# adaLN vectors computed piece by piece beside other work, norms and mixes taken block by block, in a two-layer SSD/attention trunk

## The chip, the core and the metric

The kernel runs on one core of a Trainium2 chip. The metric is the device time of one execution in microseconds (us), the median of several runs. Engines are named as in the profile: PE (matrix products), PEld (its weight loads), DVE, ACT and POOL (elementwise work), SP (issues the transfers); PEq, DVEq and so on are their instruction queues.

## The reference

A trunk of two layers over 512 tokens of width 1024, in float32. `c` is one conditioning vector.

```
c_act = silu(c)
for l in range(2):
    ada = c_act @ w_ada[l] + b_ada[l]                 # 1024 -> 6144
    sh1, sc1, g1, sh2, sc2, g2 = split(ada, 6)
    h = rms_norm(x, norm1_g[l]) * (1 + sc1) + sh1
    z, xbc, dt, q, k, v, gate_s, gate_a = split(h @ w_in[l])
    y_ssm = mamba2(z, conv(xbc), dt) @ w_ssm_out[l]
    y_att = diff_attention(q, k, v) @ w_attn_out[l]
    x = x + g1 * ((sigmoid(gate_s)*y_ssm + sigmoid(gate_a)*y_att) @ w_out[l])
    h = rms_norm(x, norm2_g[l]) * (1 + sc2) + sh2
    x = x + g2 * (relu(h @ w_ff1[l])**2 @ w_ff2[l])
return rms_norm(x, final_g)
```

## The kernel before

Everything is kept transposed: `x` is 8 blocks of 128 channels by 512 tokens. All large weights come as **units** of 1024x256 (1 MB each) in one stream, in the order of their use: bc (units 0 to 3), xs (4 to 11), gates, z and ssm-out, qkv, attention-out (AO, 4), out (WO, 4), feed-forward (FF, 4 rounds of 8: four units up, four down). 80 units a layer. SP loads a unit into `raw`, ACT rounds it into `w_hi` (`convert`), POOL computes the rest `w_lo` (`low`, four instructions), and PE does 48 matmuls of 512 columns: for each of 8 k blocks and each of 2 column blocks j, hi x hi, hi x lo and lo x hi (`unit_rows`). The raw, w_hi, w_lo and PSUM buffers have two slots, so `low` of unit n+2 follows its `convert`, which waits until PE has finished unit n. Every engine has its own program; what it does is in the written order, and semaphores join the programs. The outer loop over the layers is a loop in the program.

- **Prologue of each layer** (`start`): params and dt weights are loaded after the layer before has ended. ACT squares the 8 blocks of x, DVE adds them (`norm_sums`), PE sums over partitions (L424), POOL takes the power (L1478), PE spreads it (L430). Then the 24 adaLN pieces (1 MB each): DVE multiplies every other one by `c_act` and adds (L1130 and seven of L1134), and PE sums the columns of the result (L454); PE does the rest as row products out of `raw` (L448), whose rows ACT copies out (L772) and PE turns (L462). Then `norm` on DVE and ACT: `pre` (L1090), `h_hi` (L749), `h_lo` (L1095) for 8 blocks, with the dt product on PE (L471 to L473).
- **Conv** (bc and xs): for each unit ACT seeds (L791), DVE adds three taps for each of two blocks (L1187), ACT takes tanh (L797), DVE multiplies (`silu`, L1197). Before the first unit's taps DVE has the dt chain to do (L1147 to L1180: some 25 small instructions on 32 rows). In xs PE also turns the blocks (L416).
- **AO and WO**: DVE mixes the gated halves (L1430, L1433), and when all 8 blocks are mixed ACT and DVE split them into hi and lo; after WO all 8 blocks of x are summed, then squared, then added up, then normed.
- **FF**: ACT takes relu and its square, DVE squares again and forms `op_lo` (L1455, L1458) in the first half of a round; in the second half DVE adds to x (L1464).
- **End**: the last norm writes `y_out` (L1090), and one transfer of 2 MB takes it out.

## Time and profile before

| what | us |
|---|---|
| median of 3 runs | 2995.1 (2992.75 to 2997.93) |
| profiled execution: its own time | 3004.83 |
| profiled execution: span | 3003.0 |
| PE busy | 2574.0 |
| DVE busy | 1322.4 |
| POOL busy | 1086.1 |
| ACT busy | 960.4 |
| mean granted clock of PE | 0.914 |

Stages of layer 0 in the timeline of PE: prologue to 122; bc and xs to 278; SSD, z and ssm-out to about 730; attention to 1031; AO to 1077; WO to 1127; FF from 1147 to 1496. Layer 1 begins there, its first unit at 1610, and ends at 2978. The busy times are sums over the span; a busy engine is not always the one that is waited for.

### The profile page before, as it was taken

The page shows a single profiled execution, that of the slowest core. Times are in us where ns is not written, and L with a number is a line of the kernel's source. Part 1 is how long each engine was busy: PE and PEld are TensorE (multiplying, and loading weights), DVE is VectorE, ACT ScalarE, POOL GpSimd, SP SyncE. Part 2 cuts the span into 40 slices and gives each one's busy share as a digit, 9 for nine tenths or more (in the row PEclk, how much of TensorE's full clock was granted, in tenths as well). Part 3 has the DMA queues.
Part 4 walks back from the last instruction along what each step waited for, and adds up shares of the span by engine and source line. Part 5 has one row for each costly group of instructions (what it writes and reads, how often), then busy time and mean ns, then how long its engine had stood idle before and what let it go on. Part 6 is the DMA issues. An engine that isn't in the chain of part 4 may idle for free.

```text
span 3003.0 us, 36626 instructions
## 1 busy us (share of the span) xinstructions
PE 2574.0 (86%) x12200; PEld 2051.4 (68%) x12200; DVE 1322.4 (44%) x2019; ACT 960.4 (32%) x1532; POOL 1086.1 (36%) x825
## 2 busy tenths in 40 slices
PE   5798889788888697999977988988898877799997
PEld 2586667687666476888735866676776655688885
DVE  5654434332655326333366444433335552343333
ACT  1244332322544223222212443332334442232221
POOL 0244343334322144555402443433343222445552
PEclk9899989899989698999978999998999977899998
DMA  7421111122111121222273211011121111212221
GB/s 300 175 84 70 42 42 42 66 75 77 59 55 43 43 91 64 98 98 98 97 302 116 84 57 52 32 57 70 70 91 56 43 43 57 84 71 98 98 98 56
DMA packets 34516, 251.56 MB, mean 84 GB/s; under 512 B 3824, under 2 KB 4208, under 8 KB 4976
## 3 DMA queue, kind: packets, MB, share of 16 engines
q1 hardware_dynamic: 34416, 250.30, 22.8%
q8 instruction: 54, 0.88, 0.1%
q14 instruction: 46, 0.38, 0.0%
HBM read 244.00 MB, written 6.29 MB: 83 GB/s over the span
## 4 chain that ended last, share of the span: by engine, by line
issue 51%; POOL 23%; PE 11%; POOLq 9%; DVE 3%; DMA 2%; ACT 1%; DVEq 0%; PEld 0%; PEldq 0%; ACTq 0%; SPq 0%
POOL w_lo L1485 21%; POOLq L1487 7%; PE gemm L384 3%; PE gemm L385 2%; PE gemm L386 2%; PE aux L448 2%; DMA raw<-stream 2%; POOL y_tok L1526 1%; POOL smalls L1478 1%; DVE conv L1187 1%; POOL xdt L1517 1%; POOLq L1522 1%; PE aux L416 0%; POOLq L1518 0%; DVE pre L1090 0%
## 5 line engine op out<-in xcount | busy, mean ns | idle before, releaser
L1485 POOL TENSOR_TENSOR w_lo<-raw,w_hi 128x512 fp32r<-128x512 f32 x704 | 963.9, 1399 | 1590.0 <-ACT w_hi L732 1588.6
L384 PE MATMUL gemm<-h_hi,w_hi 128*128 128x512 f32 x1536 | 647.3, 421 | 37.9 <-POOLq L1487 10.1
L732 ACT ACTIVATE w_hi<-raw 128x2048 fp32r<-128x2048 f32 x176 | 336.6, 1914 | 939.9 <-PE gemm L386 849.3
L385 PE MATMUL gemm<-h_lo,w_hi 128*128 128x512 f32 x1536 | 614.1, 400 | 0.0
L386 PE MATMUL gemm<-h_hi,w_lo 128*128 128x512 f32 x1536 | 613.3, 399 | 0.0
L384 PEld LDWEIGHTS gemm<-h_hi,w_hi 128*128 128x128 f32 x1536 | 298.5, 194 | 135.5 <-issue 59.9
L384 PE MATMUL gemm<-op_hi,w_hi 128*128 128x512 f32 x896 | 362.4, 404 | 26.6 <-POOLq L1487 23.0
L385 PE MATMUL gemm<-op_lo,w_hi 128*128 128x512 f32 x896 | 359.5, 401 | 0.0
L386 PE MATMUL gemm<-op_hi,w_lo 128*128 128x512 f32 x896 | 358.3, 400 | 0.0
L385 PEld LDWEIGHTS gemm<-h_lo,w_hi 128*128 128x128 f32 x1536 | 298.8, 195 | 69.6 <-issue 12.0
L386 PEld LDWEIGHTS gemm<-h_hi,w_lo 128*128 128x128 f32 x1536 | 297.6, 194 | 65.4
L402 PE MATMUL gemm<-w_hi,h_hi 128*128 128x256 f32 x768 | 233.1, 304 | 1.6 <-issue 1.6
L403 PE MATMUL gemm<-w_hi,h_lo 128*128 128x256 f32 x768 | 227.6, 296 | 0.0
L404 PE MATMUL gemm<-w_lo,h_hi 128*128 128x256 f32 x768 | 227.1, 296 | 0.0
L384 PEld LDWEIGHTS gemm<-op_hi,w_hi 128*128 128x128 f32 x896 | 175.1, 195 | 67.5 <-issue 16.2
L386 PEld LDWEIGHTS gemm<-op_hi,w_lo 128*128 128x128 f32 x896 | 174.9, 195 | 37.9
L385 PEld LDWEIGHTS gemm<-op_lo,w_hi 128*128 128x128 f32 x896 | 175.2, 196 | 36.5
L1455 DVE TENSOR_TENSOR usq<-relu 128x512 f32<-128x512 f32 x64 | 93.0, 1453 | 196.7 <-ACTq L1026 191.4
L402 PEld LDWEIGHTS gemm<-w_hi,h_hi 128*128 128x128 f32 x768 | 158.9, 207 | 10.2 <-issue 9.8
L1187 DVE SCALAR_TENSOR_TENSOR conv<-gemm,cw,conv 128x511 f32<-128x511 f32 x144 | 107.8, 749 | 122.6 <-ACT conv L791 98.0
L403 PEld LDWEIGHTS gemm<-w_hi,h_lo 128*128 128x128 f32 x768 | 159.0, 207 | 0.4
L404 PEld LDWEIGHTS gemm<-w_lo,h_hi 128*128 128x128 f32 x768 | 157.9, 206 | 0.0
(171 smaller groups left out, 2861.3 us busy)
## 6 DMA issues: line engine op xcount, KB each, us to landing
raw<-stream SPq DMA_DIRECT2D x200, 1024.0 KB, 4.8
ada_raw<-stream SPq DMA_DIRECT2D x24, 1024.0 KB, 7.2
xsave<-x SPq DMA_DIRECT2D x2, 2048.0 KB, 12.6
x<-xsave SPq DMA_DIRECT2D x2, 2048.0 KB, 7.8
x<-xT SPq DMA_DIRECT2D x1, 2048.0 KB, 7.7
out<-y_out SPq DMA_DIRECT2D x1, 2048.0 KB, 6.3
dtw_raw<-dtw SPq DMA_DIRECT2D x2, 512.0 KB, 8.0
rope_cos<-ropes SPq DMA_DIRECT2D x2, 256.0 KB, 2.7
```

The lines of the kernel that those rows point to most:

```text
L384: mm(o, w_hi[:, slot, k, cols], hi[:, k, :], start=k == 0, stop=False)
L385: mm(o, w_hi[:, slot, k, cols], lo[:, k, :], start=False, stop=False)
L386: last = mm(o, w_lo[:, slot, k, cols], hi[:, k, :], start=False, stop=k == KB - 1)
L402: mm(o, h_hi[:, k, toks], w_hi[:, slot, k, :], start=k == 0, stop=False)
L403: mm(o, h_lo[:, k, toks], w_hi[:, slot, k, :], start=False, stop=False)
L404: last = mm(o, h_hi[:, k, toks], w_lo[:, slot, k, :], start=False, stop=k == KB - 1)
L448: last = mm(ab[2 + s][0:1, 0:UW], cact[:, k:k + 1], raw[:, s, k, :], start=k == 0, stop=k == KB - 1)
L732: A(w_hi[:, slot], raw[:, slot], ACT.Copy).then_inc(hi_ready, 1)
L1187: last = STT(conv[:, c, lag:S], gb[c][:, 0:S - lag], cw[:, bass.ds(block * CONV + (CONV - 1 - lag), 1)], conv[:, c, lag:S], ALU.mult, ALU.add)
L1455: TT(usq[:, j], relu[:, c], relu[:, c], ALU.mult)
L1485: gp.tensor_tensor(w_lo[:, slot, ks], raw[:, slot, ks], w_hi[:, slot, ks].bitcast(F32), ALU.subtract)
L1487: pool.drain().then_inc(lo_ready, 1)
```

## The change

The 48 adaLN pieces of the two layers leave the two prologues. Eight pieces of layer 0 (those of shift 1 and scale 1) stay in front: four are done by DVE (`ada_piece` of DVE), four by PE as products with the piece as the stationary operand (`ada_piece` of PE: 16 matmuls of one column). Ten pieces (`EARLY`) are done by DVE in the conv stage of layer 0, one after each of its first ten units; thirty (`LATE`: six of layer 0 and all 24 of layer 1) by DVE in AO and FF of layer 0, one after each unit. Each is loaded by SP in its turn among the units, after a wait for the DVE step that frees its buffer, and PE sums its columns (`ada_column`) in the middle of a later unit. A unit is now done column block by column block (`unit_column`) where its input is complete. Mixes, squares and sums of squares are done block by block as the blocks come; the next layer's parameters and dt weights are loaded and its first unit converted before the layer ends; x is read again from the input in layer 0; the output goes out in 8 transfers. The loops over layers, conv rounds and FF rounds are written out.

```diff
+EARLY = [(0, m) for m in range(8, 18)]
+LATE = [(0, m) for m in range(18, 24)] + [(1, m) for m in range(ADA)]
+N_FIRST, N_EARLY, N_LATE = len(FIRST) // 2, len(EARLY), len(LATE)
+N_LATE_AO = 2
+ADA_G2 = LATE.index((0, ADA - 1))
...
+            def unit(l, n):
+                if l * UNITS + n >= 2:
+                    sp.wait_ge(lo_ready, l * UNITS + n - 1 + LO_CREDIT)
+                load(l, n)
...
+            for n in range(N_FIRST):
+                piece(ada_pe[n], *FIRST[2 * n], pe_in[n])
+                piece(ada_first[n], *FIRST[2 * n + 1], first_in[n])
+                if n == 0:
+                    sp.dma_start(x[:], xT).then_inc(x_in, 16)
+                    load_par(0)
+                    load_dtw(0)
+            for l in range(DEPTH):
+                for n in range(U_GATE):
+                    unit(l, n)
+                    if l and n == 1:
+                        sp.wait_ge(S_["layer"], l + LAYER_CREDIT)
+                        sp.dma_start(xsave, x[:]).then_inc(x_saved, 16)
+                    if l == 0 and n == 1:
+                        piece(ada_early[0], *EARLY[0], early_in[0])
+                    elif l == 0 and n == 2:
+                        sp.wait_ge(aux_full[2], total_at(l, "start", "bank2", 0) + 1)
+                        piece(ada_early[1], *EARLY[1], early_in[1])
+                    elif l == 0 and n >= 4:
+                        m = n - 2
+                        sp.wait_ge(ada_step, step_at(N_FIRST + m - 2))
+                        piece(ada_early[m % 2], *EARLY[m], early_in[m % 2])
...
+                if l == 0:
+                    for m in range(N_LATE_AO):
+                        piece(ada_late[m], *LATE[m], late_in[m])
...
+                for n in range(U_FF, UNITS):
+                    unit(l, n)
+                    if l + 1 < DEPTH and n == U_FF + 8:
+                        sp.wait_ge(ada_read, 4)
+                        load_par(l + 1)
+                    m = n - U_FF - 2 + N_LATE_AO
+                    if l == 0 and N_LATE_AO <= m < N_LATE:
+                        sp.wait_ge(ada_step, step_at(N_FIRST + N_EARLY + m - 2))
+                        piece(ada_late[m % 2], *LATE[m], late_in[m % 2])
+                if l + 1 < DEPTH:
+                    sp.wait_ge(S_["u_lo"], total_at(l, "ff", "u_lo", 4 * 8 + U_CREDIT))
+                    load_dtw(l + 1)
+            for k in range(KB):
+                sp.wait_ge(S_["pre"], DEPTH * TOTAL["pre"] + k + 1)
+                sp.dma_start(out[:, k], y_out[:, k]).then_inc(out_done, 16)
+            sp.wait_ge(out_done, KB * 16)
...
+            def unit(l, nh, slot, hi, lo, ready_k=None, between=None):
                 open_unit(l, nh, slot)
-                for k in range(KB):
...
+                        unit_rows(slot, k, hi, lo)
+                else:
+                    unit_column(slot, 0, hi, lo)
+                    if between:
+                        between()
+                    unit_column(slot, 1, hi, lo)
...
+            def ada_piece(where, bank, c):
+                for j in range(2):
+                    for k in range(KB):
+                        last = mm(bank[:, c + j:c + j + 1], where[:, k, j * P:(j + 1) * P], cact[:, k:k + 1],
+                                  start=k == 0, stop=k == KB - 1)
+                return last
+            def ada_column(n, acc, bank, c):
+                pe.wait_ge(ada_step, step_at(n))
+                for j in range(2):
+                    last = mm(bank[:, c + j:c + j + 1], acc[:, n % 2, j * P:(j + 1) * P], ones[:, 0:1], start=True, stop=True)
+                last.then_inc(ada_out, 1)
...
+                if l == 0:
+                    for n in range(N_FIRST):
+                        pe.wait_ge(pe_in[n], 16)
+                        ada_piece(ada_pe[n], ab[3], 2 * FIRST[2 * n][1])
+                        if n == 1:
+                            norm_sum(st)
+                        if n:
+                            ada_column(n - 1, ada_acc, ab[3], 2 * FIRST[2 * n - 1][1])
+                    ada_column(N_FIRST - 1, ada_acc, ab[3], 2 * FIRST[2 * N_FIRST - 1][1])
+                    pe.drain().then_inc(ada_full, 1)
+                    norm_spread(st)
+                else:
...
+                def early(n):
+                    if l == 0 and 0 <= n < N_EARLY:
+                        if n == 0:
+                            pe.wait_ge(aux_free[2], total_at(l, "start", "bank2", 1) + AUX_CREDIT)
+                        ada_column(N_FIRST + n, ada_acc, ab[2], 2 * (EARLY[n][1] - EARLY[0][1]))
...
+                if l == 0:
+                    pe.drain().then_inc(ada_full, 1)
+                    pe.wait_ge(ada_read, 2)
...
+                def late(n):
+                    if l == 0 and 0 <= n < N_LATE:
+                        layer, m = LATE[n]
+                        bank, c = (ab[3], 2 * m) if layer else (ab[2], 2 * n)
+                        ada_column(N_FIRST + N_EARLY + n, late_acc, bank, c)
+                        if n == ADA_G2 or n == N_LATE - 1:
+                            pe.drain().then_inc(ada_full, 1)
...
+                    unit(l, U_AO // 2 + u // 2, u % 2, op_hi, op_lo, between=lambda: late(u - 2))
+                pe.drain().then_inc(ada_full, 1)
                 for u in range(N_WO):
                     def mixed(k):
-                        if u == 0:
-                            pe.wait_ge(S_["mix_lo"], st("mix_lo") + 1)
-                    unit(l, U_WO // 2 + u // 2, u % 2, h_hi, h_lo, mixed)
-                norm(st)
...
-                        unit(l, i * 4 + (U_FF // 2 + u // 2), u % 2, h_hi, h_lo, normed if u == 0 else None)
+                        n = i * 8 + u - 2 + N_LATE_AO
+                        unit(l, i * 4 + (U_FF // 2 + u // 2), u % 2, h_hi, h_lo, normed if i == 0 and u == 0 else None,
+                             (lambda: late(n)) if n >= N_LATE_AO else None)
                     for u in range(4):
...
+                             lambda: late(n))
+                        if u == 0:
+                            late(n)
...
+                if l == 0:
+                    dtw_high(l)
+                    lambdas(st)
+                    act.wait_ge(ada_full, 1)
+                    convert(l, 0, 0)
+                    normed_high(st, lambda k: ada_v[:, 0, k:k + 1])
+                    convert(l, 0, 1)
+                else:
+                    convert(l, 0, 1)
+                    normed_high(st, lambda k: ada_v[:, 0, k:k + 1])
...
                 for u in range(N_AO):
...
-                    A(h_hi[:, k], mix[:, k], ACT.Copy).then_inc(S_["mix_hi"], 1)
+                    if u < N_AO - 1:
+                        convert(l, U_AO // 2 + 1 + u // 2, u % 2)
+                        mix_high(range(2 * u, 2 * u + 2))
+                mix_high(range(KB - 2, KB))
...
                 for u in range(N_WO):
-                    convert(l, U_WO // 2 + 1 + u // 2, u % 2)
-                act.wait_ge(S_["x_sum"], st("x_sum") + 1)
-                squares_of_x(st)
+                    if u < N_WO - 1:
+                        convert(l, U_WO // 2 + 1 + u // 2, u % 2)
+                    squares_of_x(st, range(2 * u, 2 * u + 2))
...
                     for u in range(8):
                         if u < 6 or not last_round:
                             convert(l, i * 4 + (U_FF // 2 + u // 2 + 1), u % 2)
+                        if last_round and u == 6 and l + 1 < DEPTH:
+                            dtw_high(l + 1)
+                        if last_round and u == 7 and l + 1 < DEPTH:
+                            convert(l + 1, 0, 0)
+                            lambdas(st_next)
+                        if last_round and u >= 4:
+                            squares_of_x(st_next, range(2 * (u - 4), 2 * (u - 4) + 2))
...
+            def ada_piece(n, where, landed, acc):
+                dve.wait_ge(*landed)
+                for k in range(KB):
+                    if k == 0:
+                        dve.wait_ge(ada_out, n - 1 + OUT_CREDIT)
+                        TS(acc[:, n % 2], where[:, 0], cact[:, 0:1], None, ALU.mult).then_inc(ada_step, 1)
+                    else:
+                        dve.wait_ge(ada_step, n * KB + k)
+                        STT(acc[:, n % 2], where[:, k], cact[:, k:k + 1], acc[:, n % 2], ALU.mult, ALU.add)\
+                            .then_inc(ada_step, 1)
...
+            for l in range(DEPTH):
+                st = Step(l, "start")
+                if l == 0:
+                    ada_piece(0, ada_first[0], (first_in[0], 16), ada_acc)
+                    norm_add(st, range(KB))
+                    norm_mean(st)
+                    for n in range(1, N_FIRST):
+                        ada_piece(n, ada_first[n], (first_in[n], 16), ada_acc)
+                    dve.wait_ge(par_in, 16)
+                    of_params(st)
+                    dtw_low(st)
+                    take_ada(1, l, ab[3], 0, 0, 2 * KB)
+                    scales(0)
+                else:
+                    norm_mean(st)
...
+                def early(n):
+                    if l == 0 and n < N_EARLY:
+                        ada_piece(N_FIRST + n, ada_early[n % 2], (early_in[n % 2], (n // 2 + 1) * 16), ada_acc)
...
-                with dve.Fori(0, N_BC // 2) as i:
+                            early(2 * base + c // 2)
...
+                    for k in range(2 * u, 2 * u + 2):
+                        dve.wait_ge(S_["mix_hi"], st("mix_hi") + 1)
+                        TT(h_lo[:, k], mix[:, k], h_hi[:, k].bitcast(F32), ALU.subtract).then_inc(S_["mix_lo"], 1)
+                    if u < N_LATE_AO:
+                        late(u)
...
-                dve.drain().then_inc(S_["x_sum"], 1)
-                norm_sums(st)
+                        dve.drain().then_inc(S_["xb"], 1)
+                    norm_add(st, range(2 * u, 2 * u + 2))
+                norm_mean(st)
                 norm(st, lambda k: amul[:, KB + k:KB + k + 1], lambda k: ada_v[:, 3, k:k + 1])
...
+                        late(i * 8 + u + N_LATE_AO)
+                    if l == 0 and i == 0:
+                        take_ada(4, 0, ab[2], 2 * N_LATE_AO, 5 * KB, 6 * KB)
                     for u in range(4):
+                        if i == 3 and u == 3 and l + 1 < DEPTH:
+                            take_ada(5, l + 1, ab[3], 0, 0, 5 * KB)
+                            TS(g1h[:], ada_v[:, 2, :], 0.5, None, ALU.mult)
+                            scales(0)
...
+                            dtw_low(st_next)
+                            of_params(st_next)
...
                                 x[:, 2 * u + j], ALU.mult, ALU.add).then_inc(bank_free[u % 2], 1)
+                            if i == 3:
+                                dve.drain().then_inc(S_["xb"], 1)
+                        if i == 3:
+                            norm_add(st_next, range(2 * u, 2 * u + 2))
+                        late(i * 8 + 4 + u + N_LATE_AO)
                     settle()
                 dve.drain().then_inc(S_["layer"], 1)
...
+            for l in range(DEPTH):
                 st = Step(l, "start")
+                if l:
+                    low(l, 0, 0)
                 rsqrt(ms, rs, st, "ms", "rs")
-                low(l, 0, 0)
+                if l == 0:
+                    low(l, 0, 0)
                 low(l, 0, 1)
```

## Rows read from the trace of the kernel before

**Rows 1.** The page: busy us (share of the span) xinstructions; the chain's shares by engine.
```profile
PE 2574.0 (86%) x12200; PEld 2051.4 (68%) x12200; DVE 1322.4 (44%) x2019; ACT 960.4 (32%) x1532; POOL 1086.1 (36%) x825
...
issue 51%; POOL 23%; PE 11%; POOLq 9%; DVE 3%; DMA 2%; ACT 1%; DVEq 0%; PEld 0%; PEldq 0%; ACTq 0%; SPq 0%
```
**Rows 2.** Windows: stretch, its us, busy us and count by engine, PEclk, DMA share, GB/s.
```profile
5.00:10.00 5.00, 0.00 (x0) 0.00 (x0) 0.00 (x0) 0.00 (x0) 0.00 (x0) 1.00 0.99 421
...
1147.00:1496.00 349.00, 349.00 (x1535) 288.83 (x1535) 129.09 (x108) 97.58 (x100) 172.59 (x120) 1.00 0.25 90
1496.00:1610.00 114.00, 77.07 (x331) 38.55 (x330) 68.02 (x138) 21.79 (x36) 6.33 (x6) 0.81 0.64 246
```
**Rows 3.** Timeline of PE: what ends its long gaps; start, us, instruction, idle before.
```profile
122.12 0.79 PE L384 MATMUL gemm<-h_hi,w_hi 128*128 128x512 f32 x1 [5.07 <-POOLq L1487]
...
150.77 0.79 PE L384 MATMUL gemm<-h_hi,w_hi 128*128 128x512 f32 x1 [5.04 <-DVE conv L1187]
...
1081.74 0.77 PE L384 MATMUL gemm<-h_hi,w_hi 128*128 128x512 f32 x1 [4.27 <-DVE h_lo L1438]
...
1138.81 1.86 PE L424 MATMUL aux<-first,ss 128*128 128x1 f32 x8 [11.95 <-DVEq L1076]
...
1510.97 1.86 PE L424 MATMUL aux<-first,ss 128*128 128x1 f32 x8 [14.57 <-DVEq L1076]
...
1609.63 0.79 PE L384 MATMUL gemm<-h_hi,w_hi 128*128 128x512 f32 x1 [5.06 <-POOLq L1487]
...
2985.59 1.87 PE L424 MATMUL aux<-first,ss 128*128 128x1 f32 x8 [7.81 <-DVEq L1076]
```
**Rows 4.** Timeline of DVE, prologue: a piece's additions, the norm, the dt chain.
```profile
28.09 3.61 DVE L1134 SCALAR_TENSOR_TENSOR ada_acc<-ada_raw,first,ada_acc 128x256 f32<-128x256 f32 x7
...
103.67 1.41 DVE L1090 SCALAR_TENSOR_TENSOR pre<-x,amul,aux 128x512 f32<-128x512 f32 x2 [0.18 <-issue]
...
115.29 0.75 DVE L1095 SCALAR_TENSOR_TENSOR h_lo<-pre,ada,h_hi 128x512 fp32r<-128x512 f32 x1
...
120.68 1.48 DVE L1149 TENSOR_SCALAR dt_s<-dt_e 32x512 f32<-32x512 f32 x1 [3.94 <-ACT dt_e L784]
```
**Rows 5.** Timeline of POOL: the power of the second norm of layer 0.
```profile
1141.00 1.01 POOL L1478 TENSOR_TENSOR smalls<-smalls 128x4 f32<-128x4 f32 x1 [6.10 <-DVEq L1079]
```
**Rows 6.** Timeline of PE: a piece's column sums, and transposes inside the conv stage.
```profile
61.43 0.61 PE L454 MATMUL aux<-first,ada_acc 128*128 128x1 f32 x4
...
220.90 1.03 PE L416 MATMUL aux<-con,xsf 128*128 128x128 f32 x8
221.69 0.48 PE L384 MATMUL gemm<-h_hi,w_hi 128*128 128x512 f32 x1
```
**Rows 7.** Timeline of DVE: first and last work of one unit of bc.
```profile
178.16 0.75 DVE L1187 SCALAR_TENSOR_TENSOR conv<-gemm,cw,conv 128x511 f32<-128x511 f32 x1 [3.67 <-ACT conv L791]
...
183.92 1.30 DVE L1197 SCALAR_TENSOR_TENSOR bct<-ctanh,conv 128x512 f32 x2 [0.25 <-issue]
```
**Rows 8.** All instructions of the taps' line: ns min/median/max, first and last start.
```profile
L1187 DVE SCALAR_TENSOR_TENSOR conv<-gemm,cw,conv x144: 746/749/753, 144.8 to 1763.5; 128x511 f32<-128x511 f32 x48, 128x510 f32<-128x510 f32 x48, 128x509 f32<-128x509 f32 x48
```
**Rows 9.** Timelines of POOL and DVE: in the conv, z and feed-forward stages.
```profile
188.27 5.06 POOL L1485 TENSOR_TENSOR w_lo<-raw,w_hi 128x512 fp32r<-128x512 f32 x4 [5.83 <-ACT w_hi L732]
...
509.34 5.95 POOL L1485 TENSOR_TENSOR w_lo<-raw,w_hi 128x512 fp32r<-128x512 f32 x4 [11.45 <-ACT w_hi L732]
...
514.10 1.74 DVE L1311 SCALAR_TENSOR_TENSOR zt<-zt,zh 128x512 f32<-128x512 f32 x1 [1.22 <-ACTq L898]
...
1259.55 1.37 DVE L1455 TENSOR_TENSOR usq<-relu 128x512 f32<-128x512 f32 x1 [4.41 <-ACTq L1026]
...
1264.39 1.62 DVE L1458 TENSOR_TENSOR op_lo<-usq,op_hi 128x512 fp32r<-128x512 f32 x1
```
**Rows 10.** The end on DVE's timeline; transfers: count, KB each, us from issue to landing.
```profile
2990.96 5.36 DVE L1090 SCALAR_TENSOR_TENSOR y_out<-x,con,aux 128x512 f32<-128x512 f32 x8 [3.30 <-PE aux L430]
...
rope_cos<-ropes SPq DMA_DIRECT2D x2, 256.0 KB, 2.7
```

More of the change, by code:

```diff
@@ L238, in build @@
         ident = con[:, K_ID:K_ID + P]
-        first = small("first", 2 + 3 * KB)
-        ones, cact, g1h = first[:, 0:2], first[:, 2:2 + 2 * KB], first[:, 2 + 2 * KB:2 + 3 * KB]
+        first = small("first", 2 + 2 * KB)
+        ones, cact = first[:, 0:2], first[:, 2:2 + 2 * KB]
+        g1h = small("g1h", KB)
         ada = small("ada", 6 * KB)
@@ L417, in transposes, with norm_sum @@
                 return last
-            def norm(step):
+            def norm_sum(step):
                 pe.wait_ge(S_["ss"], step("ss") + 1)
@@ L483, in dt_to_tokens @@
                     st.end()
-                with pe.Fori(0, N_BC // 2) as i:
+                def early(n):
[3 more added lines that the diff above has]
+                        ada_column(N_FIRST + n, ada_acc, ab[2], 2 * (EARLY[n][1] - EARLY[0][1]))
+                for i in range(N_BC // 2):
                     for slot in range(2):
-                        unit(l, i + U_BC // 2, slot, h_hi, h_lo)
+                        unit(l, i + U_BC // 2, slot, h_hi, h_lo, between=lambda: early(2 * i + slot - 2))
                 def turn_xs(i, s):
@@ L736, in full, with squares_of_x @@
                 return ab[b]
-            def squares_of_x(step):
-                for k in range(KB):
+            def squares_of_x(step, ks, new=True):
+                for k in ks:
                     step("sq")
+                    if new:
+                        act.wait_ge(S_["xb"], step.at("xb", k) + 1)
                     if k >= 2:
@@ L1064, in dve_program, with norm_add @@
             dve.drain().then_inc(ready, 1)
-            def norm_sums(step):
-                for k in range(KB):
+            def norm_add(step, ks):
+                for k in ks:
                     dve.wait_ge(S_["sq"], step("sq") + 1)
@@ L1079, in norm_sums, with take_ada, scales @@
                 dve.drain().then_inc(S_["ms"], 1)
+            def ada_piece(n, where, landed, acc):
+                dve.wait_ge(*landed)
+                for k in range(KB):
+                    if k == 0:
[5 more added lines that the diff above has]
+                            .then_inc(ada_step, 1)
+            def take_ada(nth, l, bank, c, first, last):
+                dve.wait_ge(ada_full, nth)
+                dve.wait_ge(par_in, (l + 1) * 16)
+                TT(ada[:, first:last], bank[:, c:c + last - first], par[:, C_BADA + first:C_BADA + last], ALU.add)
+                dve.drain().then_inc(ada_read, 1)
+            def scales(m):
+                scale_at, norm_at = ((1, C_N1), (4, C_N2))[m]
+                STT(amul[:, m * KB:(m + 1) * KB], ada_v[:, scale_at, :], 1.0,
+                    par[:, norm_at:norm_at + KB], ALU.add, ALU.mult)
+                settle()
             def norm(step, mul, shift):
@@ L1218, in xs_round @@
                             silu(step, d, xsf[:, d])
+                        if c % 2:
+                            early(N_BC + 2 * i + c // 2)
                 xs_round(0, True)
-                with dve.Fori(1, N_XS // 2) as i:
+                for i in range(1, N_XS // 2):
                     xs_round(i, False)
+                if l == 0:
+                    take_ada(2, l, ab[2], 0, 2 * EARLY[0][1], 2 * LATE[0][1])
+                    TS(g1h[:], ada_v[:, 2, :], 0.5, None, ALU.mult)
                 with dve.Fori(0, GROUPS) as g:
```

278 lines of the change are left out of this document (122 added, 156 removed).

## The prediction

> **What bounds the kernel now.** I read the page first, then PE's gaps in its timeline, then windows over the stages. The page has PE busy for 86% of the span, and the chain is for half of it PE's own issue [rows 1]. The windows show why: in the feed-forward stage PE is busy for all of 349.0 us with 1535 matmuls, 0.227 us each, so a unit of 48 costs 10.9 us and nothing but fewer products could shorten it [rows 2]. So time can only be won where PE stands still or does small work. The largest such places are the two prologues: PE's first unit starts at 122.12, and between the last unit of layer 0 (1510.97 - 14.57 = 1496.40) and the first of layer 1 (1609.63) lie 113.2 us [rows 3]. Smaller ones are the joints AO/WO (4.27 us idle), WO/FF (11.95 us and the norm behind it) and the end (7.81 us and what follows) [rows 3]. The sum is made against the span of 3003.0 us (own time 3004.83); the median of the runs, 2995.1, is 9.7 lower, and I subtract from the median.
>
> **Prologue of layer 0.** Transfers run at 421 GB/s when queued [rows 2]. Ahead of the last first piece stand 11.5 MB (constants, x, parameters, eight pieces), 27 us and a start of about 2: it lands near 30, the third transfer of pieces (the second for PE) near 17. PE's product with a piece is 32 passes; at 0.1 to 0.2 us a pass (0.61 for 4, 1.86 for 8) [rows 3, 6] I take 5.6 us, so PE's norm sum comes near 23 and DVE goes on at 24.4. Then three pieces at 0.35 + 3.61 us [rows 4] lead to 36.3, the last column sums and a drain to 37.3, the spread to 39.6. The norm from its first `pre` to its last `h_lo` took 103.67 to 116.04, 12.4 us [rows 4]: 52.0. POOL now works on the first `w_lo` meanwhile, and `h_lo` reads two tiles of SBUF; for that (below) I add 2.5. Norm ready at 54.5 instead of 116.04: **-61.5** (bounds -64, nothing for the last point, and -55, PE's passes all at 0.23 us).
>
> **The dt chain** hides most of what else is won there. It began 4.6 us after the norm (120.68), because ACT converted two units first; now one is converted ahead of the norm, and it begins about 3.2 after. The third unit of bc waits for the taps behind this chain (150.77, released by DVE) [rows 3, 4], so that the first units start five microseconds earlier for nothing. **-1.4 in each layer, -2.8.**
>
> **Ten early pieces in conv.** DVE's work on a bc unit goes from 178.16 to 185.22, 7.1 us [rows 7]; a piece adds 4.0 [rows 4]: 11.0, against PE's 10.9 and a column. That fits, if nothing stretches. But the additions of a piece read both the piece and the accumulator from SBUF. The taps, which read one operand from PSUM, never leave 746 to 753 ns [rows 8], and beside them a `low` takes 5.06 us. `zt<-zt,zh`, the same instruction with both operands in SBUF, took 1.74 us beside POOL where 128x512 takes 0.65 without it (1.30 for two), and POOL's four took 5.95 instead of 5.06 [rows 7, 9]. So each addition that meets one of POOL's four instructions costs about 1.05 us more, up to 4.2 a piece. And they will meet: POOL starts its `low` 2 us after PE ends a unit, just when a DVE that is late for one unit is in its piece; once DVE is late the pattern feeds itself, because 11.0 + 4.2 = 15.2 is more than PE's 11.4 (12.3 in xs, with the transposes). Ten pieces at 4.2 are 42 us; DVE's slack over the ten units is 4 x 0.4 + 6 x 1.8 = 12. Bounds 0 and +30; I take the upper half, because the dt chain makes DVE late from the first unit: **+18**.
> By the Trainium skill ("SBUF — State Buffer", Who interferes with whom) a DVE instruction with two SBUF inputs contends with a GpSimd instruction that reads SBUF, and the one issued second waits for the whole of the first; by that rule, the trace agrees with 1.74 us, and the rule speaks against these pieces standing beside `low`. By the same section one with a single SBUF input outside the two-port modes does not contend, which the 746 to 753 ns of the taps bear out.
>
> At the end of conv PE also waits for DVE's `take_ada` before SSD: a drain and a round trip, **+1.2**.
>
> **Forty column sums inside units.** Each is 4 passes of one column on a loaded 128x128 block: 0.61 us in the row, 0.40 by the transposes inside conv (0.79 for 8) [rows 6]. They hide behind nothing. 40 x 0.52 = **+20.8** (16 to 24). Two drains in FF, which no row prices (0 to 1.5 us each): **+1.4**.
>
> **Late pieces on DVE in FF.** In a first half DVE begins 2.5 us after PE ends a unit and needs 6.5 us (1259.55 to 1266.01) [rows 9], then 4.0 for a piece: done at 12.9, while POOL's next `low` starts at 11.4 + 2.0 = 13.4. It just fits and costs 0. Were DVE half a microsecond later, the third rival would hold. In a second half DVE has only 1.5 us to do. SP loads a piece behind a unit and waits for DVE's step two pieces back; what is queued behind it is the raw load of the next unit, needed some 10 us later. 0.
>
> **AO/WO.** The eighth block is split about 3 us after PE's end but needed 9.5 us into the next unit, so the idle 4.27 goes, and so does the slow start: WO took 1081.74 to 1126.86, 45.1 against 43.6 [rows 3]. A new drain costs some 0.8. Twice 5.0: **-10.0**.
>
> **WO/FF.** PE ended at 1126.86 and POOL took the power at 1141.00 [rows 3, 5]. Now only the last block is left: add 0.8, square 0.6, add up 0.7, PE sum 1.9, power at 1131.4. But ACT converts the second FF unit after the last squares (to 1130.3), and in POOL's written order that unit's `low`, 5.1 us, stands ahead of the power: 1135.6. So the power is 5.3 us earlier, not 9.6. This stall was covered before by the sums. **-10.6 for two** (bounds -8 and -19).
>
> **Layer 1.** The norm ended 6.08 us ahead of the first unit (as 116.04 and 122.12), at 1603.5, 107.1 after PE's end [rows 3, 4]. Now: 2.4 to the sum of squares, 5.4 from PE's sum to the norm's first instruction (2985.59 to 2990.96 at the end) [rows 3, 10], 12.4 of norm, 0.6 for one meeting with POOL: 20.8. Here POOL's `low` of unit 0 is done a unit earlier. **-86.3**. The 24 pieces of this layer are in the terms above.
>
> **End.** The gap of 7.81 shrinks to 2.4; the tail from the last `y_out` (2996.3) to 3003.0, 6.7 us, becomes a 256 KB transfer, 2.7 and 0.3 [rows 3, 10]: **-9.1**.
>
> Sum: -61.5 - 2.8 + 18 + 1.2 + 20.8 + 1.4 - 10.0 - 10.6 - 86.3 - 9.1 = -138.9, so a span of 2864 and a median of **2856 us**.
>
> **Rivals.**
> *No lock in conv (15%).* DVE catches up, pieces meet POOL seldom. For it: 11.0 < 11.4. Against: rows 9, and the late start. 18 and 2.5 fall away: 2836.
> *PE pays more for a column (8%).* The wait and the change from 512 columns to one break its stream of weight loads; a column costs 1.2 us instead of 0.52. For it: 8 passes after idle took 1.86 [rows 3]. Against: the transposes in conv. +27: 2883.
> *The meetings reach FF (8%).* Conv at its upper bound (+12), and in the 16 first-half units of FF each piece runs into the next `low`, 3 us over a slack of 1: +32. 2900.
> *Slower (2%).* SP's order: a raw load stuck behind the wait for a DVE step, so that `convert` starts late. To decide, 38 queued loads must cost PE over 3.7 us each, which needs DVE some 14 us behind. Lateness in conv feeds back through this, but no row shows SP near it: above 3001.
> *Part of it doesn't happen (5%).* The end of layer 0 stays long since DVE has the scales, the dt rest and the parameters to do before the last x; I find them done 5 us before PE's column. If not: +5 to 10, about 2864.
> The forecast has 62%, its own range 2843 to 2870. 2830 to 2886 takes in the first, second and fifth, and leaves out some 2 in 10 with the bounds. A measurement of this kernel tells 0.2% (6 us) from no change. Faster 0.97, within 0.2% 0.01, slower 0.02.
>
> **What would show it.** First unit of PE near 55, third of bc near 88; conv's `ada_acc` additions at 1.4 to 1.7 us where they meet POOL and 0.48 elsewhere; bc and xs units of 13 to 14 us; in FF of layer 0 units of 11.4 and additions of 0.48 in first halves; POOL's power after WO right behind a `low`; 21 to 22 us between the layers; 256 KB transfers at the end. Wrong would be: PE waiting for POOL or for transfers in FF, or columns above 0.7 us.

## The result, and the profile after

The changed kernel takes 2833.2 us, the median of 4 runs (2814.8 to 2835.8), beside 2996.5 for the kernel before on the same chip: a ratio of 0.9443, 95% interval 0.9402 to 0.9484. Run again with five timed rounds it was 0.9448 (0.9435 to 0.9461). The prediction said 2856; the profiled execution has a span of 2831.2 us (own time 2833.0) against 3003.0, so 171.8 us less where the sum had 138.9. The medians lie 163.3 us apart: the profiled execution of the kernel before was 8 us slower than its median, so a part of the difference between the traces is that.

The page after: busy us and instructions by engine, the chain's shares. They answer to [rows 1].

```profile
span 2831.2 us, 33328 instructions
...
PE 2488.8 (88%) x11928; PEld 2036.0 (72%) x11928; DVE 1471.0 (52%) x2183; ACT 950.2 (34%) x1508; POOL 1108.3 (39%) x825
...
issue 37%; POOL 21%; PE 18%; DVE 8%; POOLq 8%; ACT 4%; DVEq 2%; ACTq 1%; DMA 0%; SPq 0%
```

The span had 36,626 instructions before. PE has 272 matmuls fewer (and PEld as many weight loads), but the total fell by 3298: most of what went is not counted as busy on any engine. That is the first sign of what the prediction lacked.

PE's timeline after, what ends its gaps, as in [rows 3]:

```profile
6.22 6.96 PE L459 MATMUL aux<-first,ada_pe 128*128 128x1 f32 x32 [6.22 <-DMA ada_pe<-stream]
...
34.96 6.96 PE L459 MATMUL aux<-first,ada_pe 128*128 128x1 f32 x32
...
89.08 0.76 PE L438 MATMUL gemm<-h_hi,w_hi 128*128 128x512 f32 x1 [7.10 <-DVE conv L1317]
...
110.85 0.61 PE L467 MATMUL aux<-first,ada_acc 128*128 128x1 f32 x4 [1.22 <-DVE ada_acc L1203]
...
1064.39 2.08 PE L505 MATMUL aux<-con,smalls 128*128 128x128 f32 x8 [5.11 <-POOL smalls L1648]
...
1437.41 1.05 PE L497 MATMUL aux<-first,ss 128*128 128x1 f32 x8 [3.05 <-DVEq L1187]
...
1485.11 0.76 PE L438 MATMUL gemm<-h_hi,w_hi 128*128 128x512 f32 x1 [7.00 <-DVE conv L1317]
...
2817.94 1.73 PE L497 MATMUL aux<-first,ss 128*128 128x1 f32 x8 [2.68 <-DVEq L1187]
```

The third unit of layer 0 begins at 89.08 instead of 150.77, that of layer 1 at 1485.11 instead of 1638.20, and the gap at the end is 2.68 instead of 7.81. PE's product with a piece took 6.96 us instead of the 5.6 assumed, and the last three of the four, one after another with nothing but sums between them, set the end of the adaLN sums. In three of the first units PE then waits 1.2 us before a column sum for the additions on DVE (`ada_acc`). These are one unit's additions on DVE, and POOL's `low` beside them:

```profile
104.48 6.32 DVE L1203 SCALAR_TENSOR_TENSOR ada_acc<-ada_early,first,ada_acc 128x256 f32<-128x256 f32 x7
110.72 4.91 DVE L1317 SCALAR_TENSOR_TENSOR conv<-gemm,cw,conv 128x511 f32<-128x511 f32 x6
```

```profile
106.23 5.71 POOL L1655 TENSOR_TENSOR w_lo<-raw,w_hi 128x512 fp32r<-128x512 f32 x4 [9.13 <-ACT w_hi L822]
```

Seven additions took 6.32 us where the prologue had 3.61 [rows 4], POOL's four 5.71 where they had 5.06 [rows 9]. The six taps took 4.91, one behind the other; before they were spread over 5.5 us.

Four windows after (columns as in rows 2): one group of the state-space stage in layer 0, the feed-forward, the boundary between the layers, and one group in layer 1:

```profile
383.46:434.63 51.17, 45.62 (x200) 33.48 (x201) 22.98 (x33) 17.43 (x27) 22.00 (x20) 0.93 0.12 41
1069.00:1434.00 365.00, 364.79 (x1648) 302.48 (x1648) 286.47 (x348) 104.84 (x111) 186.40 (x124) 0.99 0.45 165
1434.36:1456.20 21.84, 12.02 (x42) 7.86 (x42) 15.56 (x25) 8.14 (x10) 5.92 (x5) 0.77 0.51 192
1776.63:1831.12 54.49, 48.74 (x200) 35.66 (x201) 23.17 (x33) 17.38 (x27) 21.17 (x20) 0.87 0.11 38
```

The feed-forward is still PE's own work, 365 of 365 us, and longer by the column sums. (A group is one pass of the loop over `GROUPS` in the state-space stage, four in each layer.) The two groups do the same with as many matmuls, and one takes 3.3 us more: the granted clock is 0.87 instead of 0.93.

By stages, measured from starts on PE's timeline, the 171.8 us are: up to the third unit of layer 0, -61.7; conv, +11.3; state-space stage, -9.1; z and what follows up to attention, -2.8; attention, -4.6; AO and WO, -5.2; WO/FF, -5.6; feed-forward, +15.6; the boundary up to the third unit of layer 1, -91.1; conv, -1.1; state-space, +10.2; z, -3.2; attention, -4.7; AO and WO, -6.3; WO/FF, -5.6; feed-forward, +1.4; the end, -9.3. Attention and z are in stages that the sum left at nothing.

### The profile page after: what moved, and what is told of

Read it like the earlier page. It is cut to its first block, busy times and chain, and to the rows that moved or that the text cites. A ratio compares the mean times of both kernels' runs of the same rounds, so it can differ in the third digit from the quotient of the medians.

```text
span 2831.2 us, 33328 instructions
## 1 busy us (share of the span) xinstructions
PE 2488.8 (88%) x11928; PEld 2036.0 (72%) x11928; DVE 1471.0 (52%) x2183; ACT 950.2 (34%) x1508; POOL 1108.3 (39%) x825
## 4 chain that ended last, share of the span: by engine, by line
issue 37%; POOL 21%; PE 18%; DVE 8%; POOLq 8%; ACT 4%; DVEq 2%; ACTq 1%; DMA 0%; SPq 0%
POOL w_lo L1655 18%; POOLq L1657 6%; PE gemm L438 2%; PE gemm L440 2%; PE gemm L439 2%; PE gemm L427 2%; PE gemm L428 2%; PE gemm L429 2%; PE aux L489 1%; ACT probs L1055 1%; DVE conv L1317 1%; POOL y_tok L1700 1%; DVE ada_acc L1203 1%; POOL smalls L1648 1%; ACT swap L1037 1%
## 5 line engine op out<-in xcount | busy, mean ns | idle before, releaser
L1655 POOL TENSOR_TENSOR w_lo<-raw,w_hi 128x512 fp32r<-128x512 f32 x704 | 986.3, 1431 | 1449.3 <-ACT w_hi L822 1448.3
L438 PEld LDWEIGHTS gemm<-h_hi,w_hi 128*128 128x128 f32 x960 | 181.6, 189 | 51.5 <-issue 14.9
L440 PEld LDWEIGHTS gemm<-h_hi,w_lo 128*128 128x128 f32 x960 | 181.3, 189 | 38.8
L439 PEld LDWEIGHTS gemm<-h_lo,w_hi 128*128 128x128 f32 x960 | 181.5, 189 | 37.0
L439 PE MATMUL gemm<-op_lo,w_hi 128*128 128x512 f32 x512 | 200.7, 392 | 0.0
L440 PE MATMUL gemm<-op_hi,w_lo 128*128 128x512 f32 x512 | 200.7, 392 | 0.0
L427 PEld LDWEIGHTS gemm<-h_hi,w_hi 128*128 128x128 f32 x576 | 115.6, 201 | 69.5 <-issue 47.6
```

The costliest lines, as they stand in the source:

```text
L427: mm(o, w_hi[:, slot, k, cols], hi[:, k, :], start=k == 0, stop=False)
L438: mm(o, w_hi[:, slot, k, cols], hi[:, k, :], start=k == 0, stop=False)
L439: mm(o, w_hi[:, slot, k, cols], lo[:, k, :], start=False, stop=False)
L440: last = mm(o, w_lo[:, slot, k, cols], hi[:, k, :], start=False, stop=k == KB - 1)
L1655: gp.tensor_tensor(w_lo[:, slot, ks], raw[:, slot, ks], w_hi[:, slot, ks].bitcast(F32), ALU.subtract)
```

## The experiments

My theory: what the sum lacks is the written-out loops. The diff turns the loop over layers, the loops over units of conv and feed-forward, and SP's loops over units into plain Python loops, and the sum priced nothing for it. The rival: the surplus comes from the granted clock or from chance. (The first turns out to be a part of the answer.)

**The loops alone.** The kernel before, with those loops written out on all engines:

```diff
-            with dve.Fori(0, DEPTH) as l:
+            for l in range(DEPTH):
...
-                with dve.Fori(0, N_BC // 2) as i:
+                for i in range(N_BC // 2):
```

> The kernel before with its layer loop, its loops over units of the conv and of the feed-forward, and SP's loops over units written out, as the change has them, and nothing else of the change. If the part of the gain that the sum did not have comes from the written-out loops: attention 253.5 instead of 258.7 us a layer, the six conv taps of a B/C unit 4.93 instead of 5.94 us, the gaps of 0.16 to 0.2 us between a unit's taps gone, 12 to 18 us in all, a ratio near 0.995. If it comes from TensorE's granted clock or from chance: these stretches as before, a ratio within 0.2% of 1.

Measured: 2971.3 us against 3000.8, ratio 0.9906 (0.9888 to 0.9924): 29.5 us, more than expected. The span is 2969.4, 33.6 less. Attention took 252.6 instead of 257.2 and 252.3 instead of 257.2, the third unit of layer 0 began 3.35 us earlier and conv won another 1.6. In attention the groups of DVE and ACT show where it comes from (busy us, mean ns | idle before them). Before:

```profile
L1373 DVE TENSOR_TENSOR aux<-aux,con 128x128 f32<-128x128 f32 x62 | 15.5, 295 | 20.4 <-PE aux L648 15.3 <-issue 4.9
...
L965 ACT ACTIVATE probsT<-aux 128x128 f32<-128x128 f32 (+3 forms) x32 | 14.0, 438 | 15.1 <-PE aux L416 10.5 <-issue 4.6
```

With the loops written out:

```profile
L1373 DVE TENSOR_TENSOR aux<-aux,con 128x128 f32<-128x128 f32 x62 | 15.4, 295 | 18.7 <-PE aux L648 15.5 <-issue 0.5
...
L965 ACT ACTIVATE probsT<-aux 128x128 f32<-128x128 f32 (+3 forms) x32 | 14.0, 438 | 13.3 <-PE aux L416 10.3
```

The busy time is the same to 0.1 us; the idle time put down to issue is gone. The taps of one unit of bc, before and written out:

```profile
178.16 0.75 DVE L1187 SCALAR_TENSOR_TENSOR conv<-gemm,cw,conv 128x511 f32<-128x511 f32 x1 [3.67 <-ACT conv L791]
179.09 0.75 DVE L1187 SCALAR_TENSOR_TENSOR conv<-gemm,cw,conv 128x510 f32<-128x510 f32 x1 [0.17 <-issue]
...
181.09 0.75 DVE L1187 SCALAR_TENSOR_TENSOR conv<-gemm,cw,conv 128x511 f32<-128x511 f32 x1 [0.35 <-issue]
```

```profile
173.69 4.93 DVE L1187 SCALAR_TENSOR_TENSOR conv<-gemm,cw,conv 128x511 f32<-128x511 f32 x6 [4.51 <-ACT conv L791]
```

In attention neither engine has a loop of its own; what changed there is that the layer number is a constant. In that stage of layer 0 the trace of the kernel before has 110 register instructions on DVE and 119 on ACT, and none on either with the loops written out.

So the edit is worth its time, more than expected, and chance is ruled out. The granted clock is not: these are the windows of attention in layer 0, before and written out (columns as in rows 2).

```profile
773.66:1030.86 257.20, 193.45 (x970) 150.79 (x969) 137.05 (x341) 112.05 (x291) 58.17 (x46) 0.83 0.12 42
754.56:1007.12 252.56, 188.76 (x969) 148.02 (x968) 137.86 (x341) 112.05 (x291) 58.48 (x46) 0.85 0.12 42
```

The stage is 4.6 us shorter, and so is PE's busy time, for as many matmuls, at a granted clock of 0.85 instead of 0.83; PE's idle time is 63.8 in both. Over the whole span PE's busy time fell from 2574.0 to 2550.7 us with the same 12,200 matmuls: 23.3 of the 33.6 us. The granted clock was 0.921 to 0.925 in the five executions and 0.915 to 0.920 in the nine of the kernel before beside them. The loops are the cause, since nothing else was changed, but most of what they cost shows as matmuls at the lower clock and not as idle time of PE; how much of it the shorter gaps give directly, no run separates. Taken stage by stage, 24.3 of the 33.6 us lie outside the state-space stage; in that stage the groups of layer 0 are 11.3 shorter at a higher granted clock, those of layer 1 are 2.0 longer.

**DVE's loops alone** (the layers, the units of conv and of the feed-forward; the other engines keep theirs).

> The kernel before with only DVE's loops written out (its layers, the units of the conv, the units of the feed-forward); the loops of the other engines stay. With all engines written out the conv gained 4.3 us, attention 4.6 us a layer, and the span 33. If the cost is DVE's register instructions alone: the conv's 4.3 us are all there and attention's too. If each engine in the chain pays for its own (DVE's waits put down to issue in attention were 4.9 us, ACT's 4.6): the conv's 4.3 us, and 2 to 2.5 us of attention a layer; in all 9 to 15 us, a ratio near 0.996, the state-space stage apart.

Measured: 2982.6 against 3001.3, ratio 0.9951 (0.9935 to 0.9967): 18.7 us by the medians, 14.7 by the ratio, where the second branch had 9 to 15. Conv has all of its gain (from the third unit to the second half of the last one 110.9 us, with all engines 110.8, before 111.8; the third unit begins 5.3 us earlier than before). Attention has 2.8 of 4.6 us in layer 0 and 4.3 of 4.9 in layer 1; in layer 0 DVE's wait for issue is down to 0.5 and ACT's stays:

```profile
L965 ACT ACTIVATE probsT<-aux 128x128 f32<-128x128 f32 (+3 forms) x32 | 14.0, 437 | 14.4 <-PE aux L416 9.8 <-issue 4.5
```

So each engine has its own idle time before short instructions, and DVE's loops are most of the price. In the two traces the other engines' loops don't show at all outside the state-space stage: 27.3 us are gone there with DVE's alone, 24.3 with all.

**The change once more**, for the clock.

> The changed kernel once more. If the group period of the state-space stage (51.2 or 54.8 us for three groups in each layer) goes by the granted clock of the run and not by the code, the same code shows both levels in different layers or executions, and single times lie up to 20 us apart around 2833 us. If it goes by the code, layer 0 is at 51.2 and layer 1 at 54.5 us again, and all times are within 3 us of 2833.

Measured: 2836.6 us (2833.0 to 2838.0, so not all within 3 us), and the profiled execution has a span of 2831.2 again, with every group of the state-space stage within 0.15 us of the first: 51.2 in layer 0 (52.0 the first), 54.5 in layer 1. Two traces of the same code agree. That doesn't mean that the code settles it: one of the first four runs of it took 2814.8 us at a granted clock of 0.933 instead of 0.925 to 0.927, and a kernel below took 2808.6 to 2833.9 at 0.940 to 0.928. The next kernel moves the start of layer 1's groups.

**More work for PE.** The change, with the two matmuls of one column sum in layer 0's feed-forward issued eleven times over:

```diff
-                for j in range(2):
+                for j in range(2 * 11 if n == N_FIRST + N_EARLY + 12 else 2):
+                    j %= 2
```

> The changed kernel with the two small matmuls of one column sum in layer 0's feed-forward issued eleven times over, into the same place: twenty matmuls more of TensorE, about 5 us. If the groups of the state-space stage have their length from the code alone: layer 1's groups at 54.5 us as in the change, all that follows 5 us later, 2842. If their length goes by when the stage starts against the granted clock: some groups of layer 1 at 50 to 52 us, so the result lies 3 to 14 us under 2842, although TensorE has more to do.

Measured: ratio 0.9487 (0.9469 to 0.9505), 2846.1 us. The feed-forward grew by 9.3 us, not 5. The trace has two passes for each of these matmuls, 44 with the four of the column itself. These are three windows: the first 24 passes, the other 20, and the thirteen matmuls of 512 columns behind them (the counts take in a neighbour at an edge):

```profile
1227.62:1230.14 2.52, 2.52 (x25) 2.52 (x23) 2.38 (x6) 1.91 (x1) 0.33 (x1) 1.00 0.74 312
1230.14:1234.56 4.42, 4.42 (x23) 4.42 (x23) 1.22 (x2) 0.00 (x0) 4.42 (x4) 0.50 0.69 241
1234.56:1240.25 5.69, 5.69 (x14) 4.44 (x15) 3.75 (x8) 0.00 (x0) 0.29 (x1) 0.50 0.60 203
```

The first passes start 0.112 us apart, so forty of them would be 4.5 us, as expected. Then the granted clock falls to half, although PE has not been idle: the passes come 0.213 apart, and the thirteen matmuls take 5.7 us instead of 3.0. The whole is 6.9 us instead of the column's 0.4, and 2.7 behind it: 9.3.

Layer 1's groups stayed at 54.5, so this shift of 20 us moved nothing there, and the expectation of a shorter result fell. But in this execution (the slowest of the five) PE's first unit began 2.3 us later (62.37), and the groups of layer 0, which stand ahead of the edit, came out differently from the same instructions:

```profile
231.31:283.52 52.21, 46.60 (x200) 34.11 (x201) 22.95 (x32) 17.86 (x29) 17.18 (x16) 0.91 0.06 21
283.52:336.90 53.38, 46.27 (x200) 32.91 (x200) 24.59 (x33) 17.59 (x28) 21.73 (x20) 0.94 0.11 39
336.90:391.64 54.74, 47.67 (x200) 33.92 (x201) 23.71 (x33) 17.54 (x28) 21.69 (x20) 0.91 0.11 38
391.64:443.24 51.60, 44.57 (x200) 31.93 (x200) 23.64 (x33) 17.47 (x27) 21.70 (x20) 0.97 0.12 41
```

Over all traces a group takes 48 to 56 us. Whether the later start did it is not shown: the next run has another first group at the same start. What decides stays open.

**Power first.** In POOL's program the power after WO stands ahead of the last `low`:

```diff
                 for nh in range(U_AO // 2 + 1, U_FF // 2 + 1):
                     low(l, nh, 0)
+                    if nh == U_FF // 2:
+                        rsqrt(ms, rs, st, "ms", "rs")
                     low(l, nh, 1)
-                rsqrt(ms, rs, st, "ms", "rs")
```

> In POOL's program the power that ends the norm after WO stands before the low half of the second feed-forward unit instead of behind it. If TensorE waits 5.1 us there for nothing but that power: 4 to 5 us a layer, 8 to 10 in all, a ratio near 0.9965 of the change. If the low half that is now later is what TensorE waits for next: nothing, within 0.2%.

Measured: 2817.5 us, ratio 0.9385 (0.9372 to 0.9398), 19 under the change. The start of the feed-forward is 2.7 and 3.0 us earlier relative to WO's end, not 4 to 5; another 10.3 us come from layer 1's state-space groups, which now took 50.1, 51.5, 51.8 and 54.5 us, and layer 0's first lost 2.8. That first group stands ahead of the edit, and PE starts it at the same time in both; the change, and this kernel:

```profile
228.99:281.07 52.08, 46.48 (x200) 34.09 (x201) 22.94 (x32) 17.87 (x28) 17.20 (x16) 0.92 0.06 21
228.98:283.84 54.86, 49.23 (x201) 36.01 (x201) 23.02 (x32) 17.91 (x28) 17.27 (x16) 0.87 0.06 20
```

The granted clock is at half when the group starts in both, and stays so until 237.7 in the change and 243.6 here. So neither the instructions nor their start settle a group's clock, and only the 5.7 us at the feed-forward are the edit's for certain. PE's timeline and POOL's show why 2.7:

```profile
1060.00 1.87 PE L497 MATMUL aux<-first,ss 128*128 128x1 f32 x8 [2.56 <-DVEq L1187]
1063.26 2.07 PE L505 MATMUL aux<-con,smalls 128*128 128x128 f32 x8 [1.39 <-POOL smalls L1648]
1068.81 0.77 PE L427 MATMUL gemm<-h_hi,w_hi 128*128 128x512 f32 x1 [3.48 <-DVE h_lo L1234]
```

```profile
1062.19 1.01 POOL L1648 TENSOR_TENSOR smalls<-smalls 128x4 f32<-128x4 f32 x1 [7.61 <-DVEq L1190]
1063.17 4.94 POOL L1655 TENSOR_TENSOR w_lo<-raw,w_hi 128x512 fp32r<-128x512 f32 x4
```

PE's wait for the power fell from 5.11 to 1.39, 3.7 us. Then `low` runs beside the norm, and PE's wait for the first `h_lo` grew from 2.47 to 3.48. The prediction's step (the power stuck behind a `low`) was right, and its gain if freed is 2.7 to 3.0 us a layer.

**Partial sums in PSUM.** Pieces 0 to 3 and 6 to 9 of the early ten add up in a PSUM bank that is free there; the last addition writes SBUF:

```diff
-            def ada_piece(n, where, landed, acc):
+            def ada_piece(n, where, landed, acc, part=None):
...
+                out = acc[:, n % 2] if part is None else part
...
-                        STT(acc[:, n % 2], where[:, k], cact[:, k:k + 1], acc[:, n % 2], ALU.mult, ALU.add)\
+                        STT(acc[:, n % 2] if k == KB - 1 else out, where[:, k], cact[:, k:k + 1], out, ALU.mult, ALU.add)\
```

> Eight of the ten early adaLN pieces keep their partial sums in a PSUM bank that is free in the conv, and only the last addition of a piece writes SBUF. If the additions and POOL's low halves hold each other up at SBUF: seven additions of a locked unit go from 6.3 back towards 3.6 us, POOL's low half from 5.6 towards 5.0, TensorE's wait of 1.2 us before each of the first units is gone, 4 to 6 us in all, a ratio near 0.998. If the additions are as long on their reads of the weights alone: 6.3 us stays and the ratio is 1 within 0.1%.

Measured: 2829.1 us, ratio 0.9416 (0.9398 to 0.9434), 7.5 under the change. Conv from the third unit took 115.6 instead of 122.6. DVE and POOL in the same unit:

```profile
101.24 3.11 DVE L1204 SCALAR_TENSOR_TENSOR aux<-ada_early,first,aux 128x256 f32<-128x256 f32 x6
104.39 0.48 DVE L1204 SCALAR_TENSOR_TENSOR ada_acc<-ada_early,first,aux 128x256 f32<-128x256 f32 x1
```

```profile
104.30 5.05 POOL L1659 TENSOR_TENSOR w_lo<-raw,w_hi 128x512 fp32r<-128x512 f32 x4 [7.66 <-ACT w_hi L822]
```

Seven additions are back at 3.6 us with `low` beside them, and `low` is back at 5.05: both engines had been held up while the running sum stood in SBUF beside the piece. This agrees with the Trainium skill ("SBUF — State Buffer", Who interferes with whom).

**Early additions cut short.** Each early piece runs only the first of its eight instructions on DVE; the rest of the products is left out.

> The changed kernel in which each of the ten early adaLN pieces runs only the first of its eight instructions on DVE: seven eighths of these products are left out, and the loads, the waits and the column sums stay. The run with sums in PSUM took 6.4 us off the first five units of the B/C part, which then were 11.38 us apart instead of 12.88. If DVE and POOL holding each other up was the whole cost of the early additions, this run gains the same 7 us in the conv (units 11.38 apart, last product of the x part 58.2 us earlier than before instead of 51), a ratio near 0.9975 of the change. If the additions cost something by their mere length as well: more, up to the 10 us that the conv lost.

Measured: 2827.4 us (2808.6 to 2833.9), ratio 0.9418 (0.9393 to 0.9444), some 9 us under the change by the ratios. Conv from the third unit took 116.7, about as little as with sums in PSUM (115.6), and the bc units were 11.4 apart. So the length of the additions costs nothing in conv; their meeting `low` in SBUF costs 6 to 7 us, and what is left over the 110.8 of the written-out kernel, 4.8, is ten column sums.

**Few column sums.** 35 of the 40 inside units are left out, their results missing (24 in layer 0's feed-forward, 2 in AO, 9 in conv).

> The changed kernel in which TensorE leaves out 35 of the 40 adaLN column sums that stand in the middle of units (their results are missing). By the sum's 0.52 us a column: 18 us less; by the trace of the change, in which the stretch of 28 columns in the feed-forward grew by 15.6 us, 19.5 us less, 13 to 14 of it in the feed-forward of layer 0. Rival, that a column fills time in which TensorE would wait: under 10 us. The group times of the state-space stage may shift by 3.5 us each on top, with the granted clock.

Measured: ratio 0.9376 (0.9356 to 0.9395), 21.6 us under the change by the ratios. By stages the feed-forward gave 11.3, AO and WO 1.1, conv 1.5; the groups of layer 1 (49.8 to 51.8 us) gave 14.8 and those of layer 0 took 6.8 more. A column in the feed-forward costs 11.3 / 24 = 0.47 us, under both figures expected; nothing hides it. In conv, where PE waited for DVE anyway, it was 1.5 / 9 = 0.17.

**Both, and no loops at all.** Power first with the sums in PSUM, and then also the remaining loops (the groups and gates of the state-space stage, ACT's conv units, POOL's units) written out.

> Power first and the partial sums in PSUM together. If the two gains lie in different stages (5.7 us at the two starts of the feed-forward, 7.2 us in the conv of layer 0) they add up: 13 us under the change, 2823, if the groups of the state-space stage run as in the change; with groups of layer 1 at 51.2 us instead of 54.6 another 3 to 10 us less, down to 2810.

> As the one before, and every loop that the change had left (groups of the state-space stage, its gates, ACT's conv units, POOL's units) written out too. If loop and register instructions cost in these stages what they did in attention (4.6 us a layer) and conv (4.3 us): 3 to 12 us more off, a ratio near 0.997 of the one before, from idle time put down to issue on DVE and ACT. If these stages wait for TensorE anyway: the same within 0.2%.

Measured: 2812.5 us, ratio 0.9382 (0.9367 to 0.9397), and 2795.0, ratio 0.9327 (0.9313 to 0.9340). In "both" each gain is in its own stage at its own size (conv 115.9, WO to feed-forward 33.3 and 33.0 instead of 36.0). The kernel without loops is the fastest, some 36 us under the change by the ratios and 17.5 under "both", more than expected: 4.5 in z of layer 0, 2.7 in attention of layer 0, 8 in the groups. In part that is the clock: attention had no loop left, and PE was busy there 3.2 us less at a granted clock of 0.89 instead of 0.87.

## Why the prediction was off

The direction and the large terms held; the time came 23 us under the forecast. That is outside the forecast's own range, 2843 to 2870; it is inside the wider one, 2830 to 2886, by the number of a rival whose mechanism did not happen (below). The step that failed is one that the sum doesn't have: the loops, a term put at nothing without a reason. The parts of the change were gone through one by one, and the diff's first lines, which turn `Fori` into `range`, were read as form. They took 29.5 us off by themselves (33.6 of span, of which 23.3 are PE's busy time, for the same matmuls at a higher granted clock). The rows that would have pointed there existed: DVE's [0.18 <-issue] in [rows 4] and [0.25 <-issue] in [rows 7]. The chain's share of issue, 51% [rows 1], would not have priced it: with the loops written out it is 30%, for a span only 1.1% shorter.

Against the kernel with written-out loops, the rest of the change is 138.2 us of span beside a sum of 138.9. That is luck and not a proof of the sum: the state-space groups took 10.5 us more in the change, which no term had, so the terms themselves made 148.7 and the two errors cancel. Term by term, against that kernel:

- *Prologue and dt chain*, -62.9: measured -58.3. The first term was mis-sized, with the norm ready at 59.2 and not 54.5: PE's product took 6.96 us instead of 5.6, the norm began 6.4 us late and then took 13.2 us instead of 12.4 + 2.5. PE's passes were 0.213 us apart, as in the half-clock window of the run with more work (there is no record of the granted clock before 53 us); that is near the bound that I had named and not taken.
- *Early pieces, their columns and `take_ada`*, +18 + 5.2 + 1.2 = 24.4: measured +13.0. The mechanism was right: additions that met `low` took up to 1.48 us, and the pattern fed itself. But a piece in it took 2.7 us more and not 4.2, and only five of the ten were in it whole, two in part (4.5 us) and the last three not at all (3.61). What ended it in xs no run isolates; a unit there is longer for PE (12.3 us instead of 11.4), and DVE's work on a unit was 6.2 us and not 7.1, the gaps of the loop gone. Its share is 6 to 7 us, not 18. The rival without a lock, at 2836, was wrong about the mechanism and nearest in the number: that is luck, for the early pieces do meet `low`, and what the sum lacked lay elsewhere.
- *Columns and drains in the feed-forward*, +16.0: measured +15.2. The column is 0.47 and not 0.52 us; the remaining 2.0 us (15.2 - 28 x 0.47) are the drains and the joints of the units, which no run separates; layer 1's feed-forward, with no columns in it, is 0.8 us longer than with only the loops written out.
- *AO/WO with its two columns*, -4.0: -5.5, and -6.5 in layer 1 without columns. *WO/FF*, -5.3: -5.65 in both, for the reason given.
- *Layer 1*, -87.7 up to its third unit: -89.0, and then +2.5 in conv, for a reason told below. *End*, -9.1: -9.1.
- *Late pieces on DVE in the feed-forward*, 0: PE waited for none of them. All instructions of the line's two later uses (ns min/median/max, first and last start):

```profile
L1203 DVE SCALAR_TENSOR_TENSOR late_acc<-ada_late,first,late_acc x210: 483/485/1480, 984.1 to 1402.3; 128x256 f32<-128x256 f32 x105
L1203 DVE SCALAR_TENSOR_TENSOR ada_acc<-ada_early,first,ada_acc x70: 483/485/1482, 90.7 to 205.4; 128x256 f32<-128x256 f32 x70
```

The late ones meet `low` too, now and then, but DVE has the time there. The rivals of dearer columns, of meetings in the feed-forward and of SP's order did not come about.

## What to carry to other kernels

A diff that writes a loop out is a change of its own, in every stage that uses the loop's variable: look for idle time put down to issue ahead of short instructions before counting the parts that the diff is about. Those rows show the place and not the price: in attention of layer 0 4.4 us of it went on DVE and 4.6 on ACT, and the stage became 4.6 us shorter, with PE's idle time as before and its clock higher. Where a DVE instruction must run beside GpSimd, let its running sum stand in PSUM: the same seven additions took 3.6 instead of 6.3 us, and `low` 5.05 instead of 5.7. Where PE is the bound, each small column sum inside a unit costs its 0.47 us, and many in a row cost more, by the clock. A wait removed ahead of a chain is worth only what the next wait leaves.

## What the runs showed of the hardware

- A wait can lower the clock and so cost more than its length. In the change PE waits 7.00 us for the third unit of layer 1; the granted clock falls to half 2.0 us into the wait, and PE's first twelve matmuls run 0.43 us apart, the lower level of 1.2 GHz, until 1490.4. With only the loops written out the wait is 3.00 us, and the first matmuls run 0.23 us apart. That is the +2.5 us above.
- One-column passes can lower the clock though PE is never idle. In the run with more work PE did 24 of them 0.112 us apart, straight behind matmuls of 512 columns at full clock; then the granted clock fell to half, the passes came 0.213 apart, and the thirteen matmuls behind them 0.43. In the prologue of the change PE did nothing but such passes from 17.9 to 43.3 us, without a pause and 0.213 apart to the last.
- A group of the state-space stage, with the same 200 matmuls, takes 51.2 us at a granted clock of 0.93 and 54.5 at 0.87. What settles it is open: the first group of layer 0, from the same instructions and the same start, took 52.1 us in the change and 54.9 with the power first. Eight groups can so move a run by up to 8 x 3.3 = 26 us, more than most single edits here; such edits have to be read from their own stage.
- Register instructions of a loop's variable cost on the engine that runs them: 0.16 to 0.5 us ahead of instructions of 0.75 us on DVE, gone when the loop is written out. Writing them out also raised the granted clock of the whole kernel, from 0.914 to 0.923 in the traces.
